# Two transformer blocks on one core: input rows and constants moved back in the queues, the first chunk multiplied in three rounds, products of zeros ahead of it

## The reference

```
h = rms_norm(x, norm_mix);  z = h @ w_in
out_a = spatial_gating(z_a, ...)         # gMLP, chunks of 128
out_b = dilated_attention(...)           # 4 heads
out_c = nsa_attention(..., compress_blocks(...), ...)   # 8 heads, 2 kv heads
x = x + concat(out_a, out_b, out_c) @ w_out
x = x + cross_attention(rms_norm(x), rms_norm(mem))
x = x + square(relu(rms_norm(x) @ w_up)) @ w_down
rms_norm(x, final_norm)
```

## Time and profile before

| | |
|---|---|
| median of 3 runs | 2602.07 us (2601.8 to 2602.39) |
| the profiled execution's own time | 2600.4 us |
| its span, first to last instruction | 2598.6 us |
| TensorE busy | 2576.3 us, 99% |
| VectorE, ScalarE busy | 1838.8 us (71%), 1361.8 us (52%) |
| bytes moved | 582.98 MB, mean 224 GB/s |

### The profile page before, as it was taken

How to read it: one execution, slowest core, us unless ns; L and a number is a source line. 1 busy time by engine, 2 the same in 40 slices (tenths; PEclk the granted TensorE clock), 3 DMA queues, 4 the chain that set the end, 5 groups by cost and what they waited for, 6 DMA issues and landing times.

```text
span 2598.6 us, 35433 instructions
## 1 busy us (share of the span) xinstructions
PE 2576.3 (99%) x13200; PEld 2173.1 (84%) x13200; DVE 1838.8 (71%) x3327; ACT 1361.8 (52%) x2613; POOL 176.9 (7%) x233
## 2 busy tenths in 40 slices
PE   8999999999999999999999999999999999999999
PEld 7999889888888888888888898888788888888887
DVE  5677665777799999676867775677866665555555
ACT  5445575655545445455766566565544444444443
POOL 1011100021100000000011100000001111000000
PEclk9999999999999999999999999999999999999999
DMA  9796665688888888866777755544577777565564
GB/s 304 236 296 184 209 202 171 188 287 278 290 284 270 277 285 271 308 191 219 237 242 236 247 175 153 156 131 153 162 233 257 255 253 224 186 195 188 188 193 161
DMA packets 315707, 582.98 MB, mean 224 GB/s; under 512 B 30176, under 2 KB 38384, under 8 KB 315408
## 3 DMA queue, kind: packets, MB, share of 16 engines
q1 hardware_dynamic: 296768, 559.94, 66.0%
q0 software_dynamic: 18480, 20.47, 3.6%
q10 hardware_dynamic: 288, 0.31, 0.0%
HBM read 574.35 MB, written 2.10 MB: 222 GB/s over the span
## 4 chain that ended last, share of the span: by engine, by line
PE 96%; DVE 1%; ACT 1%; SPq 0%; DMA 0%; issue 0%; DVEq 0%; ACTq 0%
PE ps L1838 27%; PE ps L1840 26%; PE ps L1839 26%; PE ps L1827 3%; PE ps L1828 3%; PE ps L1829 3%; PE ps L1784 2%; PE ps L1920 1%; PE ps L1890 1%; PE ps L1909 1%; DMA raw<-in_w_in 0%; DVE wlo L2495 0%; PE ps L2035 0%; ACT whi L2157 0%; PE ps L2052 0%
## 5 line engine op out<-in xcount | busy, mean ns | idle before, releaser
L2495 DVE TENSOR_TENSOR wlo<-raw,whi 128x512 fp32r<-128x512 f32 x1712 | 1098.2, 686 | 536.5 <-ACT whi L2157 534.0
L2157 ACT ACTIVATE whi<-raw 128x512 fp32r<-128x512 f32 x1712 | 982.0, 624 | 817.1 <-PE ps L1840 527.1
L1838 PE MATMUL ps<-whi,th 128*128 128x512 f32 (+1 forms) x3124 | 1230.9, 394 | 2.2 <-ACT hA L2351 1.0
L1840 PE MATMUL ps<-whi,tl 128*128 128x512 f32 (+1 forms) x3124 | 1211.2, 388 | 0.0
L1839 PE MATMUL ps<-wlo,th 128*128 128x512 f32 (+1 forms) x3124 | 1210.3, 387 | 0.0
L1838 PEld LDWEIGHTS ps<-whi,th 128*128 128x128 f32 x3124 | 586.9, 188 | 122.2 <-issue 5.1
L1840 PEld LDWEIGHTS ps<-whi,tl 128*128 128x128 f32 x3124 | 586.5, 188 | 121.7
L1839 PEld LDWEIGHTS ps<-wlo,th 128*128 128x128 f32 x3124 | 587.4, 188 | 115.7 <-issue 1.0
L2513 DVE SCALAR_TENSOR_TENSOR acc<-raw,silc,acc 128x512 f32<-128x512 f32 x480 | 343.9, 746 | 10.5 <-DMA raw<-in_w_mod 6.0
L1827 PE MATMUL ps<-th,whi 128*128 128x256 f32 x640 | 186.0, 291 | 11.0 <-DVE wlo L2495 8.1
L1828 PE MATMUL ps<-th,wlo 128*128 128x256 f32 x640 | 181.6, 284 | 0.0
(11 more groups left out here) (320 smaller groups left out, 1296.7 us busy)
## 6 DMA issues: line engine op xcount, KB each, us to landing
raw<-in_w_in SPq DMA_DIRECT2D x231, 512.0 KB, 3.9
raw<-in_w_down SPq DMA_DIRECT2D x216, 512.0 KB, 4.6
raw<-in_w_mod SPq DMA_DIRECT2D x192, 512.0 KB, 4.5
raw<-in_w_gate_up SPq DMA_DIRECT2D x176, 512.0 KB, 3.5
raw<-in_w_up SPq DMA_DIRECT2D x128, 512.0 KB, 4.6
raw<-in_w_out SPq DMA_DIRECT2D x64, 512.0 KB, 3.8
raw<-in_xattn_wkv SPq DMA_DIRECT2D x16, 512.0 KB, 3.4
raw<-in_w_in SPq DMA_DIRECT2D x16, 268.0 KB, 4.1
```

What stands on the lines that cost most here:

```text
L1838: pe.matmul(p, xh, wh[:, c, c0:n], start=a and (form != "both" or tb == 0), stop=False, skip_group_check=True)
L1840: ins = pe.matmul(p, xl, wh[:, c, c0:n], start=False, stop=z, skip_group_check=True)
L2157: self.e.activation(t.his[g % NHI][:, n * c:n * c + n], t.raws[j % NRAW][:, n * c:n * c + n], ACT.Copy).then_inc(*s.hi.up((g, c)))
L2495: self.e.tensor_tensor(t.los[j % NRAW][:, at], t.raws[j % NRAW][:, at], t.his[g % NHI][:, at].bitcast(F), ALU.subtract).then_inc(*s.lo.up( ...
```

## The change

- `load_x`: chunk 7 is issued before the last part of `xt` and before the four pieces of x.
- `take_in`: `halves_in` is cut into `high_in` (ScalarE) and `low_in` (VectorE), with a `yield` between them for piece 0 of the input.
- `multiply`: chunk 0 in three rounds over its four heads, high x high first, then those with the weights' low half, then those with the input's low half, each round with its own wait.
- `late_loads` waits for the end of the last chunk that was multiplied when it is emitted, not for piece 5.
- `compress`: a third `yield` before the first products.
- `first_products`: VectorE writes zeros to 256 columns of `xn`, and TensorE multiplies them seven times in plain float32, 256 columns each, before anything else; the first `stat`, which writes `xn`, waits for them.

```diff
@@ load_x
-            self.issue_upto(2 + min(j, 5))
+            self.issue_upto(min(2 + j, NRAW))
@@ take_in
-                self.halves_in(name, j, src, landed, op, g, gtok, sh, shtok)
+                self.high_in(name, j, src, landed, op, g, gtok, sh, shtok)
+                if name == "x" and j == 0:
+                    yield
+                self.low_in(name, j, src, op, g, sh)
@@ run
         self.start_loads()
+        bank = self.side().take()
+        self.first_products(bank, 7)
+        bank.give((s.wm, 0))
+        self.xn_after = [[(s.wm, 0)] for _ in range(4)]
         self.load_x()
...
-            self.late_loads()
+            self.late_loads(self.mark)
@@ Pool
-    def late_loads(self):
+    def late_loads(self, begun):
-        self.wait_ge(*s.tl.at(("x", 5)))
+        self.wait_all([begun])
@@ Tensor, multiply
+        if j == 0:
+            heads_at = [(pair.tile[h // 2][:, S * (h % 2):S * (h % 2) + S], slice(128 * h, 128 * h + 128)) for h in range(heads)]
+            self.wait_ge(*s.hi.at((g, 0)))
+            self.wait_ge(*s.th.at((op.name, 0)))
+            for h, (p, hs) in enumerate(heads_at):
+                pe.matmul(p, wh[:, 0, hs], op.h[:, 0, :], start=h % 2 == 0, stop=False, skip_group_check=True)
+            self.wait_ge(*s.lo.at((g, 0)))
+            for p, hs in heads_at:
+                pe.matmul(p, wl[:, 0, hs], op.h[:, 0, :], start=False, stop=False, skip_group_check=True)
+            self.wait_all(op.ready[0])
+            for p, hs in heads_at:
+                ins = pe.matmul(p, wh[:, 0, hs], op.l[:, 0, :], start=False, stop=False, skip_group_check=True)
+            ins.then_inc(*s.mm.up(j))
+            return
+    def first_products(self, bank, n):
+        t, s = self.t, self.s
+        self.wait_ge(*s.wz.at(0))
+        for _ in range(n):
+            ins = self.e.matmul(bank.tile[:, 0:256], t.xn[:, 0:128], t.xn[:, 0:256], start=True, stop=True, skip_group_check=True)
+        ins.then_inc(*s.wm.up(0))
@@ Vector
+    def first_products(self, bank, n):
+        t, s = self.t, self.s
+        self.e.memset(t.xn[:, 0:256], 0.0).then_inc(*s.wz.up(0))
```

More of the change, by code:

```diff
@@ L156, in __init__ @@
         self.out = new("out_stored")
+        self.wz, self.wm = new("first_zeros"), new("first_products")
 class Operand:
@@ L203, in same @@
         return self
-    matmul = transpose = activation = preload_act_table_set = tensor_tensor = tensor_scalar = tensor_copy = reciprocal = same
+    memset = matmul = transpose = activation = preload_act_table_set = tensor_tensor = tensor_scalar = tensor_copy = reciprocal = same
     scalar_tensor_tensor = tensor_tensor_reduce = tensor_reduce = dma_start = same
@@ L356 @@
     start_loads = load_mem_part = load_mem_rows = silu_columns = spread_rstd = mem_square = heads_direct = finish = load_xt_part = load_x_rows = late_loads = load_ctx = load_final = load_masks = load_bounds = load_qkg = skip
-    issue = halves_in = scale_in = split = mod_add = mod_total = mod_turn = mod_fold = mod_scatter = multiply = turn_scale = turn_piece = raw_piece = settle_scale = settle_halves = turn_low = stat = root = reduce_sums = skip
-    idle_products = heads_silu = roots_next = rows_out = residual_add = spatial_weights = skip
+    issue = high_in = low_in = scale_in = split = mod_add = mod_total = mod_turn = mod_fold = mod_scatter = multiply = turn_scale = turn_piece = raw_piece = settle_scale = settle_halves = turn_low = stat = root = reduce_sums = skip
+    first_products = idle_products = heads_silu = roots_next = rows_out = residual_add = spatial_weights = skip
     att_scores = att_softmax = att_cmp = att_turn = att_values = skip
@@ L2131, in silu_columns, with high_in @@
         self.e.activation(t.silc[:, :], t.cols2[:, 0:32], ACT.Silu).then_inc(*s.silc.up(0))
-    def halves_in(self, name, j, src, landed, op, g, gtok, sh, shtok):
+    def high_in(self, name, j, src, landed, op, g, gtok, sh, shtok):
         s = self.s
@@ L2479, in scale_in, with low_in @@
         ins.then_inc(*s.ts.up((name, j)))
-    def halves_in(self, name, j, src, landed, op, g, gtok, sh, shtok):
+    def low_in(self, name, j, src, op, g, sh):
         s, dv = self.s, self.e
```

## The result

The changed kernel takes 2605.31 us (median of 20 runs, 2602.29 to 2606.57), the kernel before 2601.10 (20 runs, 2600.21 to 2602.39): ratio 1.0015, interval 1.0009 to 1.0021, so slower by 4.2 us, 0.16%. The prediction said 2602.6 in a range of 2599.0 to 2605.0; the time lies above it, and the difference, +0.5 forecast, is eight times as large. The sign was right, the size was not. (4.2 us is less than the 0.2% that the prediction took as the bound of what can be told; all the same, the interval lies above 1.)

A forecast was written before the change was run, and what follows sets the result against it. TensorE was busy 2576.3 of 2598.6 us, its start bound by bytes at 389 GB/s. Start gains are given back before chunk 7, net +0.6; spread and `cb` -0.1; so 2602.07 + 0.5 = 2602.6 us, range 2599.0 to 2605.0.

The forecast's parts named there:

- The bound by bytes, the order and the yield: At the start, transfers at 389 GB/s; the yield puts piece 6 behind high 8, chunk 7's product at 30.1, 0.6 us later.
- Whatever the start has won is stopped there: Ahead of chunk 7, start -1.0, half-speed products -1.3 and small wait -0.35 us are all given back.
- signs of being wrong: Long idle ending at 20 us with piece 6 before 24; products behind the gap at 0.21; gaps from 60 us differing.
- the rule beside the sum: At TensorE's forecast 2.8 us wait before chunk 7, the skill warns of half clock after long idle gaps; sum kept +0.5.
- rival 1: Clock falls in the wait before chunk 7: 14 products cost 1.3 us, 0.45 gets through, 2603.1; chance 0.12.
- the order's own part: Queue order up to 50 us, at full clock: +0.6 at chunk 7's start, -0.1 after, so +0.5 us.
- spread and `cb` together -0.1: Around chunks 10 to 13: row scale's spread a tick later, `cb` wait of 1.84 us returning as 1.9; net -0.1.
- From there no gap before or after: From 50 us on, TensorE has no gap in either kernel, so the +0.5 us stays to the end.
- The full gain (2594.7): The wait before chunk 7 really goes, all 7.35 us won; chance 0.05, or 0.09 for a part (2600).
- Late constants: Constants landing after 64 us stop VectorE at the spatial weights' step; at 72 us +5.5 to 8, 2608; chance 0.04.
- hold anyone up at 40 to 52 us: The constants' transfers collide with awaited chunks at 40 to 52 us: +2, 2604.6; chance 0.08.
- The zeros: Before the first product, seven plain products take at most 4.2 us and end before 6.8; priced at nothing.

The follow-up runs named there:

- run 1: The changed kernel without the yield between piece 0's high and low part in `take_in`; 2598.78 us, ratio to before 0.9992.
- run 2: The kernel before with only the yield between piece 0's high and low part added; 2605.44 us, ratio 1.0015.
- run 6: The changed kernel without both yields, piece 0's and the third in `compress`; 2598.71 us, ratio to before 0.9991.
- run 8: The kernel before with chunk 7 ahead of x and the late constants moved back, without rounds, zeros and yields; 2598.80 us, ratio 0.9991.
- run 4: The changed kernel with 28 unread products ahead of chunk 7 and 12 ahead of chunk 13; 2603.45 us, ratio to before 1.0010.
- run 3: The changed kernel without the third yield in `compress`; 2605.51 us.
- run 5: The changed kernel without the third yield in `compress`, with 28 unread products ahead of chunk 7 and 22 ahead of the first compression product; 2603.21 us.
- run 7: The kernel before with the late constants moved back and nothing else; 2600.02 us, ratio 0.9995.
- run 10: A repeat of run 9's kernel, the changed kernel without both yields and with x issued behind chunk 11; 2598.71 us.
- run 9: The changed kernel without both yields, x issued behind chunk 11, sums of squares three ticks later, `heads_direct` held until the rstd spread; 2597.86 us, ratio 0.9988.

## Why the prediction failed, step by step

**The bound by bytes, the order and the yield: right.** The prediction read that `take_in`'s new yield puts piece 6 behind high 8 and that x stays ahead of chunk 8. The profile after has exactly this queue, run 1 takes the yield out and gets 6.5 us back, run 2 puts it in alone and loses 4.4. "Whatever the start has won is stopped there" holds too: runs 6 and 8 differ by 0.1 us. The prediction's own signs of being wrong came all the same, two of three: the products behind the gap come in steps of 0.21 us, and a gap behind 60 us is new.

**The step that failed** is the rule beside the sum and what was made of it in rival 1. The forecast kept full speed "by the row", a wait of 2.23 us with no fall behind it, and gave the fall a chance of 0.12 and a price of 0.45 us. Half clock shows in the profile behind two waits, most runs have a mean clock that fits it (14 of 20 at 0.998), and the falls together cost 1.9 us (run 4). Three things were wrong in it:
- A row in which a wait of 2.23 us does no harm does not show that such waits are harmless. The executions after it show falls behind 3.37, 1.74 and 1.55 us.
- The wait itself was longer than forecast, 4.06 us instead of 2.8, because TensorE had finished chunk 6 earlier (26.8 instead of 27.2) and chunk 8's weights were there at 27.9 instead of 27.1. In run 3 they came at 27.0, so 27.1 was a fair value of something that varies: 27.0, 27.6, 27.6 and 27.9 in the profiles of runs 3, 4, 5 and the changed kernel, which have the same transfers ahead of it.
- Only one fall was priced. Chunk 7 had slack of its own, as the prediction said, but it priced 14 products at half clock (1.3 us); all 24 ran so, 5.2 us instead of 2.9, and chunk 8 started at about 36.2 where the queues alone would have let it start at 34.6. The second fall, in chunk 13, has no slack behind it. That it would come was nowhere in the text, though the wait before chunk 13 was.

The Trainium skill's rule, "TensorE: Matmul & The Clock Gate", section "Why this matters for your kernels", warns of long idle gaps between bursts; this case's trace agrees (4.06 us, then 0.50), and shows falls behind shorter waits too, 1.74 and 1.55 us.

**The second step: the order's own part**, +0.5 forecast, +2.4 measured with the waits filled (run 4). It has two errors.
- At chunk 8 it was +0.6 and measured 1.1, since the weights came at 27.6 in that run and not at 27.1. From there to chunk 13 the forecast was right: "spread and `cb` together -0.1" measured 0.0 (1.1 late at chunk 8, 1.1 at chunk 13). The third yield in `compress` does hide the wait for `cb`, which without it is 2.7 us (run 3), and brings back nearly as much, as forecast (1.74 us against 1.9).
- "From there no gap before or after" was wrong: the wait before the turn, 0.9 us in the changed kernel's profile and 1.6 in run 4, is the larger part of what was missing. It goes with that yield: it is there in runs 1 and 4 and not in runs 3, 5 and 6. The trace shows the way: with the yield SyncE sends a chunk of `w_in` alone at 97.78, 3.1 us behind a chunk of compression weights, and the high half that waits for weights runs at 101.52, after the turn's first four products (101.23); in run 3 two chunks leave together at 93.75 and two high halves run from 97.72, ahead of those products (100.08). What holds SyncE back there was not followed further.

**The base** was 1.0 us high: 2602.07 is the median of three runs, 2601.1 that of twenty. It made the prediction look nearer than its difference was.

**The other rivals.** The full gain (2594.7) was out of reach, but a version without the yield shows 2.3 us of it, and x moved behind chunk 11 2.3 to 3.2. Late constants did not occur: they left from 42.35 on instead of 39.6, and the mask of the spatial weights, at 68.50, still found them there without a wait. Nor did they hold anyone up at 40 to 52 us: one high half waits for its weights until 51.85, but VectorE is at `cb` and chunk 13's low half then and comes to that chunk later. In the kernel before, the move is worth 1.1 us in the medians and 0.3 in the profiles (run 7).

**The zeros** were priced at nothing, which held by a narrow margin. The prediction took 0.30 us for a product and 4.2 us at most for seven; in the profile they are 14 records and took 5.5 us, until 6.69. In run 5 they took 6.06 us, until 7.25, and the first product follows at 7.36 without a wait, so there they were the last thing ahead of it.

## What to carry to other kernels

In a program whose queues are filled in step, a yield is a distance in every queue: before adding one, write down which instruction now stands ahead of which on each engine, and what that one waits for. Moving a transfer forward helps only if the next thing that its reader waits for isn't behind the old obstacle; here the chunk came 7.5 us earlier and the piece beside it 1.4 us later. And price a wait of TensorE with what the clock may do behind it, each such wait by itself: a single profile without a fall is one draw, and the spread of the runs sorted by their granted clock tells more. It does so where the falls are large: in the kernel before, the runs at 0.999 took 2601.1 to 2601.2 and those at 1.000 took 2600.6 to 2601.1, hardly a difference. And don't end the sum where the change ends: about 1 us of the loss (0.9 in the changed kernel's profile, 1.6 in run 4) arose near 100 us, behind weights that came late in the order of SyncE's queue.

## What the runs showed of the hardware

- The granted clock fell to 0.50 behind waits of 4.37, 4.06, 3.37, 1.95, 1.80, 1.74 and 1.55 us, and did not behind 2.32 and 2.03 us (runs 10 and 9) and 2.23 us in the kernel before. Behind the same wait for `cb`, 2.71 us long, it fell in the profile of run 3 and not in that of run 2. Ahead of the first compression product, 16 narrow ones, it fell behind 1.83 us in run 8 and not behind 1.84 us in the kernel before and 1.83 us in run 7. Run 8, with the wait ending at 44.18:

```profile
40.00:44.00 4.00, 2.35 (x11) 1.00 1.02 359
44.00:45.00 1.00, 0.82 (x17) 0.91 0.92 323
45.00:48.00 3.00, 3.00 (x8) 0.50 1.05 371
48.00:50.00 2.00, 2.00 (x10) 0.94 0.50 144
```

  So the length of the wait alone does not tell whether it falls.
- With products whose results nobody reads in the waits, the mean clock was 1.000 in 9 of 11 runs (run 4) and in all 11 (run 5). Here that was worth 1.9 us, less than taking the first wait away (6.5 us, run 1).
- Behind the plain products of zeros the first chunk ran at full speed from its first product (the four of its first round took 0.74 us in all, in steps of 0.12), where the kernel before has 14 steps of about 0.21 us; the granted clock reads 1.00 in both. In the time this does not show (runs 6 and 8).
